# A dense SwiGLU network's down projection by seven block products, in two halves of its output columns

## The reference

```python
def swiglu(x, w_up, w_down):
    g, v = jnp.split(x @ w_up, 2, axis=-1)
    return (jax.nn.silu(g) * v) @ w_down      # w_up (1024, 5632), w_down (2816, 1024)
```

## Time and profile before

| | |
|---|---|
| median of 3 runs | 1264.89 us (1263.78 to 1265.14) |
| the profiled execution, its own time | 1266.41 us |
| its span in the profile | 1264.6 us |
| PE busy over the span | 1232.7 us (97%) |
| DVE busy | 706.1 us (56%) |
| ACT busy | 424.5 us (34%) |
| POOL busy | 100.9 us (8%) |
| dense network, up to the last down product | about 209 to 424 us |

### The profile page before, as it was taken

The page is one execution under the profiler, slowest core; times in us unless marked ns, Lnnn a source line. Parts: engine busy times, 40 slices in busy tenths (PEclk is TensorE's granted clock), DMA queues, the critical chain, the costliest instruction groups (busy, mean ns, idle before and its releaser), DMA issues.

```text
span 1264.6 us, 48991 instructions
## 1 busy us (share of the span) xinstructions
PE 1232.7 (97%) x21590; PEld 1046.6 (83%) x21590; DVE 706.1 (56%) x1639; ACT 424.5 (34%) x877; POOL 100.9 (8%) x161
## 2 busy tenths in 40 slices
PE   7999999999999999999999999999999999999997
PEld 5755567878887775556799999999999999999986
DVE  6876426557866376643554555555555555554545
ACT  5516513001002142642234343333334333333332
POOL 1270020000000045011000000000000000000001
PEclk9999999999999999999899999999999999999999
DMA  9521025253442543513799999999999999999995
GB/s 372 228 83 68 1 100 215 101 199 114 188 173 94 215 188 133 208 51 133 288 385 427 424 426 424 427 426 424 426 426 427 425 426 424 427 427 424 427 426 218
DMA packets 36571, 360.95 MB, mean 285 GB/s; under 512 B 4164, under 2 KB 5828, under 8 KB 11549
## 3 DMA queue, kind: packets, MB, share of 16 engines
q1 hardware_dynamic: 33776, 354.86, 68.0%
q10 hardware_dynamic: 2156, 3.19, 0.7%
q0 software_dynamic: 576, 2.10, 0.5%
HBM read 356.77 MB, written 3.36 MB: 285 GB/s over the span
## 4 chain that ended last, share of the span: by engine, by line
PE 80%; DMA 8%; DVE 3%; SPq 1%; issue 1%; ACT 1%; POOL 0%; DVEq 0%; ACTq 0%
PE bank L2609 25%; PE bank L1951 18%; PE bank L2626 13%; PE bank L2554 6%; DMA ring<-moe_w_dram 5%; PE bank L2323 4%; DMA memT<-moe_w_dram 3%; PE bank L2595 2%; PE bank L2311 2%; PE bank L1959 2%; PE bank L2252 1%; PE bank L2340 1%; SPq L548 1%; PE bank L2645 1%; PE bank L2132 1%
## 5 line engine op out<-in xcount | busy, mean ns | idle before, releaser
L2609 PE MATMUL bank<-R,ring 128*64 128x80 f32 x11264 | 426.7, 233 | 6.5 <-DVE ring L1840 4.4
L2609 PEld LDWEIGHTS bank<-R,ring 128*64 128x64 f32 x11264 | 404.4, 137 | 13.9 <-DVE ring L1840 11.5
L1951 PE MATMUL bank<-ring 128*128 128x128 f32 (+2 forms) x1760 | 284.5, 321 | 1.6 <-ACT ring L668 0.9
L1951 PEld LDWEIGHTS bank<-ring 128*128 128x128 f32 x1760 | 239.9, 191 | 49.1 <-issue 36.6
L2626 PE MATMUL bank<-zz,ring 128*64 128x80 f32 x5632 | 224.7, 233 | 0.0
L1013 ACT ACTIVATE ring<-ring 128x1024 f32<-128x1024 f32 x160 | 169.1, 1057 | 134.3 <-PE bank L2626 134.3
L2626 PEld LDWEIGHTS bank<-zz,ring 128*64 128x64 f32 x5632 | 207.9, 137 | 0.0
L1891 DVE SCALAR_TENSOR_TENSOR zz<-zz,bank 128x80 f32<-128x80 f32 x176 | 41.9, 238 | 166.2 <-PE bank L2609 165.3
L1840 DVE COPY ring<-ring 128x1024 f32<-128x1024 f32 x160 | 109.9, 687 | 23.0 <-DMA ring<-moe_w_dram 22.8
L1018 ACT ACTIVATE sqx<-bank 128x80 f32<-128x80 f32 x176 | 41.8, 238 | 223.0 <-PE bank L2609 222.4
L1844 DVE COPY ring<-ring 128x1024 f32<-128x1024 f32 x160 | 109.8, 686 | 0.3 <-issue 0.2
(11 more groups left out here) (352 smaller groups left out, 1131.4 us busy)
## 6 DMA issues: line engine op xcount, KB each, us to landing
ring<-moe_w_dram SPq DMA_DIRECT2D x158, 1536.0 KB, 21.3
ring<-ffn_w_dram SPq DMA_DIRECT2D x11, 3072.0 KB, 10.2
ring<-w_in_dram SPq DMA_DIRECT2D x6, 2048.0 KB, 7.3
extra<-moe_w_dram SPq DMA_DIRECT2D x8, 1536.0 KB, 22.9
ring<-w_out_dram SPq DMA_DIRECT2D x4, 2048.0 KB, 7.6
ring<-w_small_dram SPq DMA_DIRECT2D x2, 3072.0 KB, 10.4
ring<-w_x_dram SPq DMA_DIRECT2D x2, 3072.0 KB, 10.8
ring<-w_in_dram SPq DMA_DIRECT2D x2, 2144.0 KB, 15.3
```

The lines of the kernel that those rows point to most:

```text
L1951: i = pe.matmul(out_ap, a, b, start=(k == 0), stop=(k == n - 1))
L2609: e = pe.matmul(pb[out_bank][c0:c0 + 64, 0:CAP], half[:, P * k + c0:P * k + c0 + 64], xg[:, k], start=(k == 0), stop=(k == KT - 1), tile_p ...
```

## The change

The down projection, too, is made as seven block products. A pair of hidden tiles (256 rows of the down weights) by 512 output columns is one such product: the gated rows are cut into four blocks of 128x128, the weights into four of 128x256, each is mixed by DVE or POOL, and PE makes seven products of 128x256 in place of eight. Its four results take four banks (`down_sums` adds them up, as `up_sums` does for the up projection). Since each bank of the four then holds two results of 256 columns, only 512 output columns fit beside the four banks of the up projection, and the work is made in two halves:

- Output columns 0 to 511 (`first_half`) are made behind the up products of every second tile.
- Columns 512 to 1023 (`second`) are made when all up products are done. The gated rows of all 22 tiles therefore stay in SBUF (`hidden_places`), and the weights of these columns are loaded again by transfers of their own (`late_weights`: pairs 0 to 4 and 10 into slot 2, pairs 5 to 9 into slot 1).

The mixes: `hidden_mixes` (four of 128x128 per pair and half, all DVE's); `down_mixes` (one of 128x512 and two of 128x256 per pair and half; POOL makes all of the first half's and seven of the second's, DVE four). One of the four mixes of the up weights (`v_hi - v_lo`) goes from DVE to POOL for tiles 2 to 21. DVE's first mix of the up weights is put ahead of the gating. The state-space work of layer 1 is cut into smaller pieces and spread over more tiles: `s5_weights` at tiles 2, 3, 4 and 13 to 17, `s5_turns` at 5 to 12, one 128x2048 operation a tile. Layer 1's first weights are asked for in another order (in3, in0, in2, in1), and its turning of `h` takes the lower half of the columns first.

The diff, cut to its core:

```diff
+PAIR_ORDER = [0, 1, 2, 3, 4, 10, 5, 6, 7, 8, 9]
+EARLY_PAIRS, TAIL_PAIRS = 5, 3
+PAIRS_BY_DVE = (0, 4, 7, 9)
+PAIRS_BY_POOL = [n for n in range(CH) if n not in PAIRS_BY_DVE]
+BLOCKS = {"P2": (0, 0), "P3": (0, 1), "P4": (1, 0), "P1": (2, 0), "P6": (2, 1), "P5": (3, 0), "P7": (3, 1)}
+BLOCK_BANKS = [[4, 5, 6, 7], [0, 2, 1, 3]]
...
-                add(f"down{g}", 4 + g, 0)
+            for half in range(2):
+                for g in range(4):
+                    add(f"down{half}_{g}", BLOCK_BANKS[half][g], 0)
...
+        def down_mixes(eng, own, c, half, place_of):
+            B11, B12, B21, B22 = range(4)
+            B, T = down_blocks(c, half), down_mixed[place_of]
+            own(eng.tensor_tensor(T[:, 0:3:2], B[:, B12:B22 + 1:2], B[:, B11:B12 + 1], ALU.subtract))
+            own(eng.tensor_tensor(T[:, 1], B[:, B22], T[:, 0], ALU.subtract))
+            return eng.tensor_tensor(T[:, 3], B[:, B21], T[:, 1], ALU.subtract)
...
+                if name == "in2_1":
+                    sp.wait_ge(sem["second_half"], EARLY_PAIRS - 1)
+                if name == "in1_1":
+                    banks.wait(sp, "down1_1")
...
-                for c in (2, 3, 0, 1) if l else range(4):
+                for c in (3, 0, 2, 1) if l else range(4):
+                    if l and c == 2:
+                        sp.wait_ge(slot_free[1], FF_SLOTS.count(1))
+                        late_weights(1, EARLY_PAIRS, CH - 1, 0, "down_late")
...
-                        item(f"ff{c}", ffn_w[c])
+                        item(f"ff{c}", ffn_w[c][:, 0:UPW + 1024])
+                    sp.wait_ge(slot_free[2], FF_SLOTS.count(2))
+                    late_weights(2, 0, EARLY_PAIRS, 0, "down_early")
+                    late_weights(2, CH - 1, CH, 1024 * EARLY_PAIRS, "down_last")
...
-                        if t in (5, 9, 10, 18):
+                        if t in (1, 4, 6, 15, 17):
...
+                    for half in range(2):
+                        act.wait_ge(sem["gated"], HT)
+                        if half:
+                            act.wait_ge(sem["h_added"], 10)
+                        banks.wait(act, f"down{half}_2")
+                        act.activation(down_parts[:, 0], ps(f"down{half}_2")[:, 0:SEQ], ACT.Copy).then_inc(sem["first_copied"], 1)
...
+            def mix_down(c):
+                pool.wait_ge(sem["first_half"], c)
+                down_mixes(pool, own, c, 0, 3).then_inc(sem["down_mixed"], 1)
...
+                    banks.wait(pool, "xout3_0")
+                    for t in range(2, HT):
+                        weights_in(pool, f"ff{t // 2}")
+                        if t >= MIXED:
+                            banks.wait(pool, f"upB{t - MIXED}")
+                        _, v_lo, _, v_hi = ff_blocks(t)
+                        pool.tensor_tensor(mixed[t % MIXED][:, 2], v_hi, v_lo, ALU.subtract).then_inc(sem["values_mixed"], 1)
+                        if t % 2 == 0:
+                            mix_down(t // 2 - 1)
+                    mix_down(CH - 1)
+                    for n in PAIRS_BY_POOL:
+                        if n < 3:
+                            banks.wait(pool, f"upB{HT - 1}")
+                        elif n == 3:
+                            banks.wait(pool, "down0_3")
+                        else:
+                            pool.wait_ge(sem["second_half"], n - 3)
+                        late_in(pool, PAIR_ORDER[n])
+                        down_mixes(pool, own, PAIR_ORDER[n], 1, n % 4).then_inc(sem["pool_mixed"], 1)
...
-                    dve.tensor_tensor(T[:, 2], v_hi, v_lo, ALU.subtract)
+                    if t < 2:
+                        dve.tensor_tensor(T[:, 2], v_hi, v_lo, ALU.subtract)
...
+                def hidden_mixes(c, place_of):
+                    A11, A21 = hT(2 * c)[:, 0:P], hT(2 * c)[:, P:2 * P]
+                    A12, A22 = hT(2 * c + 1)[:, 0:P], hT(2 * c + 1)[:, P:2 * P]
+                    S = hidden_mixed[place_of]
+                    dve.wait_ge(sem["gated"], 2 * c + 2)
+                    dve.tensor_tensor(S[:, 2], A11, A21, ALU.subtract)
+                    own(dve.tensor_tensor(S[:, 0], A21, A22, ALU.add))
+                    own(dve.tensor_tensor(S[:, 1], S[:, 0], A11, ALU.subtract))
+                    dve.tensor_tensor(S[:, 3], A12, S[:, 1], ALU.subtract).then_inc(sem["hidden_mixed"], 1)
+
+                def down_sums(half):
+                    def block(g, m0=0, m1=2):
+                        return ps(f"down{half}_{g}")[:, SEQ * m0:SEQ * m1]
+
+                    X1U4, U4U3, U3U7 = down_parts[:, 0:2], down_parts[:, 1:3], down_parts[:, 2:4]
+                    h_of = [h[:, i, HALF * half:HALF * half + HALF] for i in range(NT)]
+                    dve.wait_ge(sem["first_copied"], half + 1)
+                    banks.wait(dve, f"down{half}_2")
+                    own(dve.tensor_tensor(down_u2, block(2, 1), down_parts[:, 0], ALU.add))
+                    banks.wait(dve, f"down{half}_3")
+                    own(dve.tensor_tensor(U4U3, block(3).rearrange("p (m t) -> p m t", m=2), down_u2.unsqueeze(1).to_broadcast([P, 2, SEQ]), ALU.add))
+                    dve.tensor_tensor(down_parts[:, 3], block(3, 0, 1), down_parts[:, 2], ALU.add)
+                    own(dve.tensor_tensor(h_of[0], h_of[0], X1U4.rearrange("p m t -> p (m t)"), ALU.add))
+                    own(dve.tensor_tensor(h_of[1], h_of[1], U3U7.rearrange("p m t -> p (m t)"), ALU.add))
+                    banks.wait(dve, f"down{half}_0")
+                    dve.tensor_tensor(h_of[0], h_of[0], block(0), ALU.add).then_inc(sem["h_added"], 1)
+                    banks.wait(dve, f"down{half}_1")
+                    dve.tensor_tensor(h_of[1][:, 0:SEQ], h_of[1][:, 0:SEQ], block(1, 0, 1), ALU.add).then_inc(sem["h_added"], 1)
...
+                        mixes = mix_weights(t + 2) if t + 2 < HT else iter(())
+                        next(mixes, None)
...
-                        own(dve.scalar_tensor_tensor(hT[:, 2 + t % 2], th[:, t % 2], 1.0, g_of, ALU.add, ALU.mult))
-                        dve.scalar_tensor_tensor(hT[:, t % 2], hT[:, 2 + t % 2], 0.5, v_of, ALU.mult, ALU.mult).then_inc(sem["gated"], 1)
...
-                        if t in (7, 15, 16, 17):
+                        own(dve.scalar_tensor_tensor(hT(t), th[:, t % 2], 1.0, g_of, ALU.add, ALU.mult))
+                        dve.scalar_tensor_tensor(hT(t), hT(t), 0.5, v_of, ALU.mult, ALU.mult).then_inc(sem["gated"], 1)
+                        if t % 2:
+                            dve.wait_ge(sem["first_half"], t // 2)
+                            hidden_mixes(t // 2, 2)
+                        for _ in mixes:
+                            pass
+                        if t in S5_WEIGHTS_AT:
                             next(weights, None)
-                        if 9 <= t < 13:
+                        if t in S5_TURNS_AT:
                             next(turns, None)
-                        if t == HT - 1:
+                    for n, c in enumerate(PAIR_ORDER):
+                        if n == 2:
+                            banks.wait(dve, "down0_3")
+                        if n >= 3:
+                            dve.wait_ge(sem["second_half"], n - 2)
+                        hidden_mixes(c, n % 3)
+                        if n in PAIRS_BY_DVE:
+                            if n >= 4:
+                                dve.wait_ge(sem["second_half"], n - 3)
+                            late_in(dve, c)
+                            down_mixes(dve, own, c, 1, n % 4).then_inc(sem["dve_mixed"], 1)
+                        if n == 4:
+                            down_sums(0)
+                        if n == CH - TAIL_PAIRS:
                             conv_diagonals(1)
-                    add_in("down")
+                    down_sums(1)
...
-                    pe.wait_ge(sem["h_added"], added + 2 * i + (2 if k1 > 4 else 1))
+                    upper = k1 > 4
+                    pe.wait_ge(sem["h_added"], added + (2 * upper + i + 1 if name == "mix_T" else 2 * i + upper + 1))
...
...
...
-                    def down_products(t):
-                        c, mt = t // 2, t % 2
...
...
+
+                    def down_part(half, block, c, place_of, t_of, last=False):
+                        A11, A21 = hT(2 * c)[:, 0:P], hT(2 * c)[:, P:2 * P]
+                        A12, A22 = hT(2 * c + 1)[:, 0:P], hT(2 * c + 1)[:, P:2 * P]
+                        B, S, T = down_blocks(c, half), hidden_mixed[place_of], down_mixed[t_of]
+                        a, b = {"P1": (A11, B[:, 0]), "P2": (A12, B[:, 2]), "P3": (S[:, 3], B[:, 3]), "P4": (A22, T[:, 3]),
+                                "P5": (S[:, 0], T[:, 0]), "P6": (S[:, 1], T[:, 1]), "P7": (S[:, 2], T[:, 2])}[block]
...
+                        return pe.matmul(ps(nm)[:, SEQ * m:SEQ * m + SEQ], a, b, start=first, stop=last, skip_group_check=True)
+
+                    def first_half(c):
+                        last = c == CH - 1
+                        pe.wait_ge(sem["gated"], 2 * c + 2)
```

(47 more changed lines are left out.)

101 lines of the change are left out of this document (75 added, 26 removed).

## The result

The changed kernel takes 1269.22 us (median of 13 runs, 1264.22 to 1271.92), against 1264.42 (13 runs, 1263.47 to 1268.46) before: the ratio is 1.0033 with a 95% interval of 1.0019 to 1.0047. It is 0.3% slower, where the forecast was 1260.0 and faster, and the time lies just above the range. The profiled execution took 1271.84 us (span 1269.9), 5.4 more than that of before.

The account below looks back on a forecast made before the run. PE was taken to bound the dense stage, so its saved instructions are saved time: -8.8 + 1 + 3 - 0.3 = -5.1 us, off the median 1264.9 gives 1259.8, rounded 1260; range 1255.5 to 1268.

Parts of the forecast that it names:

- The saving on PE (-8.8): Down products in the dense stage: 308 instructions of 256 columns take 66.9 us instead of 75.7, saving 8.8 us.
- DVE in the turns: Dense-stage pairs carrying turns: 13.5 us of DVE work per pair without POOL, against PE's 15.5.
- the meetings with POOL: Dense stage: DVE operations with two SBUF inputs lose at most 3.2 us per pair beside POOL; 2.2 taken.
- Stalls of PE: 1 us: Dense stage up to the last up product: PE waits 1 us for DVE, range 0 to 6.4.
- the slack: Dense stage: DVE may be 2.7 us late before PE waits for mixes of the next tile but one.
- I take 3 us of stalls: Second half, behind the last up product: PE waits 3 us for mixes, range 0.8 to 9.
- at most 11 us, of which half: Second half: POOL's 21 operations hold DVE up by at most 11 us; half, 5.5, was taken.
- the 4 us in hand: Second half: DVE has 28.5 us for 24.5 us of work, so 4 us to spare.
- The ends (-0.3): Turn from the last down product to layer 1: the last sum has 256 columns, saving 0.3 us.
- The late weights: Second half's last weight transfer arrives in time, no stall; as a rival, 1 to 3 us at the seventh pair.
- POOL's 128x512 at 1.4 us: POOL's mixes of 512 columns: taken as 1.4 us each, between 0.73 and 1.44.
- The rival on the other side: Stage and second half: complete DVE-POOL exclusion, both wait in turn; 1286 us, with half of it 1272; chance 0.14.

Follow-up runs that it names:

- experiment 4: Changed kernel with all down-projection mixes, both halves and both engines, cut to one column; stage 202.63 us, whole time not usable.
- Experiment 2: Changed kernel with ACT's two Sin operations moved ahead of tiles 16 and 18 instead of 15 and 17; 1266.07 us, ratio 1.0011 to the kernel before.
- experiment 1: Changed kernel with POOL's seven pairs of second-half down mixes cut to one column; stage 205.5 us, second half 38.97 us, whole time not usable.
- experiment 8: Like experiment 5, but DVE mixes six second-half pairs instead of four, the other five plain; 1263.2 us, ratio 0.9980 to the kernel before.
- experiment 3: Changed kernel with the seven second-half pairs that POOL mixed multiplied plainly, without mixes; 1261.95 us, ratio 0.9977 to the kernel before.
- experiment 5: Changed kernel with POOL's seven second-half pairs multiplied plainly and ACT's two Sins ahead of even tiles; 1260.1 us, ratio 0.9965 to the kernel before.
- experiment 6: Changed kernel with 13 idle products put where PE waited for mixes behind the last up product; 1268.18 us, ratio 1.0025 to the kernel before.
- experiment 7: Changed kernel with the up weights' mix v_hi - v_lo back on DVE for all tiles; 1268.76 us, ratio 1.0045 to the kernel before.

## Why the prediction was wrong

**The saving on PE (-8.8): right.** 15.5 us per pair were forecast; 15.53 stand in the trace, and experiment 4 measured -9.3 for the whole stage with the ends.

**DVE in the turns: right.** Pairs with turns cost DVE about what was worked out, and PE was held up there by 0.4 us in all. Of the meetings with POOL, the forecast had 2.2 us per pair. Five lines (L1758, L1760, L1761, L1889, L1890) lost about 17 us over ten pairs by their mean durations (for instance 898 - 685 ns, 20 times, for L1760), 1.7 us each, and small operations of the state-space weights come on top. This term had its right size in the first part.

**"Stalls of PE: 1 us" in the first part: wrong, 4.2.** Experiment 4 has 164.29 us there without mixes, after 168.52. PE's rows place it: pairs start every 15.53 us but for four, which take 0.16, 0.22, 2.03 and 1.81 more. The last two are those of tiles 15 and 17. The step that failed here is the one that named the slack: PE was taken to need DVE first for the mixes of the next tile but one, with 2.7 us in hand. What came due first were the gated rows of the odd tile, for which PE has just one up product (6.25 us) from the tile's own end, since two up products now stand together. Tile 15's ended at 334.6 (the pair's row starts at 328.31); DVE came to its sums 3.5 us later, and sums and gating, with the table load in them, took 4.3 to the product at 342.36: 3.5 + 4.3 - 6.25 is 1.5, about the wait of the row (1.39). The prediction had seen the table loads (1.28 each) and set them against a slack that was not the one in question. Experiment 2 took back 3.0 us with that one edit (2.2 on the mean of the traces), and experiment 1 shows that about 1 us of the wait was one meeting with POOL that another execution doesn't have.

**"I take 3 us of stalls" in the second half: wrong, about 10.** This is the term that decides. After's 49.27 us stand against 38.97 with POOL's mixes cut (experiment 1) and 38.34 with all cut (experiment 4). Two other traces with after's mixes in this half give 47.87 and 47.24, so the term is 9 to 11 us. The mechanism was the one named, the size was off twice. First, a meeting was priced as 0.4 us for 256 columns and 0.8 for 512, from the earlier trace rows: the price was scaled with DVE's width. But there POOL's operations were of 256 columns (0.72 us), and what DVE loses is what POOL's operation has still to run: with a 128x512 of POOL it is 1.05 us even for an operation of 128 columns. This is the smaller error: six such meetings cost 6.3 us where 0.8 each gives 4.8, and the meetings with 256 columns came to 0.44 on the mean, nearly the 0.41 foreseen. Second, and this is the step that failed: "at most 11 us, of which half" took every second meeting to be harmless. 19 of 21 were not. DVE was busy for 41.35 of the 47 us, mostly with two inputs in SBUF, so that nearly every operation of POOL met one. Twice one signal started both: the end of a pair's products (`second_half`) releases DVE's hidden mixes and POOL's down mixes for later pairs together, at 399.64 and 399.69 (row above) and again at 419.93 and 419.97. DVE lost 12.0 us (41.4 against 29.4), more than the whole of the bound. With the 4 us in hand, 12 lost make 8; the waits that PE shows are 5.9 us, and the slower clock lies on top.

The place was off too. The sum had PE wait from the sixth pair on. 4.1 of the 5.9 us stand before it: 1.18 at the last first half, 0.24, 0.59 and 2.04 at the first, second and fifth pair.

**The clock: not in the sum.** It fell twice, behind waits of 2.04 and 1.85 us. Two traces with after's mixes in this half and no fall took 47.57 and 47.24 us against 49.27, so its price is some 1.7 to 2.0 us, by one trace each; PE's rows themselves were 3.3 us longer. In all traces with a fall in the second half (after, experiments 2 and 8) it stands behind a wait of 1.85 us or more, and where there were no such waits it stayed away (experiments 1, 3, 4, 5 and 6). But experiment 7 had waits of 1.51 and 2.50 us and the full clock throughout: such a wait did not bring it every time.

**The ends (-0.3): about right,** 2.07 us from PE's first turn of `h` to layer 1's first product, against 2.35 before by the same rows. **The late weights: right.** PE never waited for one of them; POOL did once, for 0.73 us. **POOL's 128x512 at 1.4 us: right on the mean** (1460 and 1434 ns beside DVE in the first part; the shortest took 1.26 us).

**The rival on the other side was the true one** in its mechanism: exclusion of the two engines, decisive from 9.1 us of stalls on, with 5 of them in the second half. It stood at 0.14 because it was priced as a complete exclusion everywhere, 1286 or half of that. Its middle value, 1272, doesn't follow from its own terms: half of the 21 us gives 1275, half of the 30 us of stalls 1271. It came about in the second half, where DVE was hardly ever idle and the slack was 4 us; in the first part the meetings cost DVE half of the possible 3.2 us, about as forecast. Against the sum: -8.8 and -0.3 were forecast and measured as -9.3, +1 became +4.2, +3 became +10.9 with the clock, which is +5.8, the stage's own change. That the stage is also where the median's 4.8 us come from is inferred: the stage was seen in one execution of either kernel.

**What stays open.** After's thirteen executions spread over 7.7 us, before's over 5.0. After's six above 1270 us report a mean granted clock of 0.988 to 0.990, the four below 1268 us one of 0.992 to 0.995. That the two go together is all that this shows; whether the falls in the second half are missing in the faster executions was not seen, since only the execution of 1271.84 us has a trace. Why the clock fell behind the waits of after and not behind the longer one of experiment 7 is open as well.

## What to carry to other kernels

Before an engine is given work beside another, ask how busy the other is and what releases both: where it is seldom idle, or where one signal starts them together, count every meeting, each at what is left of the helper's operation and not in proportion to the other's width. Slack is to be measured at the consumer that comes due first, which a change of order can swap, as here from the mixes of a later tile to the gated rows of the tile just done. And a saving of an eighth on the engine that sets the time is soon eaten by its preparation: the plain product for part of the work was the faster kernel.

## What the runs showed of the hardware

A DVE operation of 128x128 with two SBUF inputs takes 0.28 us alone and up to 1.36 beside POOL's 128x512. POOL loses by such meetings too: its 128x512 takes 1.26 us at the least, 1.45 at most in the second half, and 2.10 us at 281.75, where it starts while DVE's L1362 (128x2048, two SBUF inputs) has still 0.97 us to run. The granted clock of PE was at 0.50 to 0.52, the lower level, for some microseconds behind waits of about 2 us in an otherwise dense stage (after at 407 and 415 us, experiment 8 at 399), and stayed at 1.00 behind a wait of 2.50 us in experiment 7. With idle products in the waits it stayed at 1.00 (experiment 6, one trace); since experiment 7 shows the full clock without them, that they did it is not shown, and the kernel was not measurably faster.
